# A transformer pair of blocks with expert routing: one 64-column product a token in place of two of 32, and the sum of the two halves moved off TensorE

## The reference

```
v1, i1 = top_k(s1, 16); v2, i2 = top_k(s2, 16)      # 8 heads, 128 keys each
sv, si = top_k(v1[:, None] + v2[None, :], 16)
expert = e1 * 128 + e2;  gate = softmax(sv)
a   = gelu(x . exp_u[expert])
out = sum over heads and picks of  gate * a * exp_v[expert]
```

## Time and profile before

| | |
|---|---|
| median of 3 runs | 3306.38 us (3305.8 to 3314.76) |
| profiled execution, its own time | 3306.54 us |
| its span | 3304.8 us |
| TensorE products busy | 3179.6 us, 96% |
| VectorE busy | 2340.2 us, 71% |
| ScalarE busy | 1256.1 us, 38% |
| chain that ended last | PE 67%, DVE 17%, DMA 10%, issue 4%, ACT 1% |
| read from HBM | 814.00 MB, 248 GB/s |

### The profile page before, as it was taken

The page is one execution under the profiler, slowest core; times in us unless marked ns, Lnnn a source line. Parts: engine busy times, 40 slices in busy tenths (PEclk is TensorE's granted clock), DMA queues, the critical chain, the costliest instruction groups (busy, mean ns, idle before and its releaser), DMA issues.

```text
span 3304.8 us, 71646 instructions
## 1 busy us (share of the span) xinstructions
PE 3179.6 (96%) x31390; PEld 2836.8 (86%) x31390; DVE 2340.2 (71%) x2685; ACT 1256.1 (38%) x1135; POOL 388.2 (12%) x284
## 2 busy tenths in 40 slices
PE   7999999999999989988989999999999999999998
PEld 4777768899999979988879998888888888888887
DVE  8596145799999877777779877578667766555554
ACT  2010143445444434333434444444443444443332
POOL 0276000000011222232212000200000000000000
PEclk8999999999999989999999999999999999999999
DMA  9657795546678988888788875556555566565553
GB/s 411 250 224 294 291 387 213 171 179 242 202 269 305 342 327 316 314 335 311 293 287 315 317 262 196 198 197 203 191 197 199 173 209 202 198 201 201 202 202 116
DMA packets 105301, 821.57 MB, mean 249 GB/s; under 512 B 12394, under 2 KB 14458, under 8 KB 15552
## 3 DMA queue, kind: packets, MB, share of 16 engines
q1 hardware_dynamic: 86112, 700.49, 58.4%
q0 software_dynamic: 16656, 115.53, 9.1%
q10 hardware_dynamic: 2304, 2.10, 0.2%
HBM read 814.00 MB, written 4.06 MB: 248 GB/s over the span
## 4 chain that ended last, share of the span: by engine, by line
PE 67%; DVE 17%; DMA 10%; issue 4%; ACT 1%; POOL 0%; ACTq 0%; DVEq 0%; SPq 0%; POOLq 0%
PE psW L587 17%; PE psW L588 17%; PE psW L589 17%; DVE ring L1191 7%; PE psW L585 7%; DMA ring<-wst_dram 4%; DMA arena<-urow_dram,rs 3%; DMA proj<-vrow_dram,rs 3%; DVE arena L1668 1%; PE psM L729 1%; PE psW L729 1%; PE psM L883 1%; PE psM L658 1%; ACT ring L2028 1%; DVE proj L1722 1%
## 5 line engine op out<-in xcount | busy, mean ns | idle before, releaser
L1191 DVE SCALAR_TENSOR_TENSOR ring<-ring 128x2048 f16<-128x2048 f32 x526 | 1200.3, 2294 | 522.8 <-ACT ring L2028 521.2
L2028 ACT ACTIVATE ring<-ring 128x2048 f16<-128x2048 f32 x526 | 1000.8, 1907 | 937.2 <-PE psW L589 776.5
L587 PE MATMUL psW<-h_act,ring 128*128 128x256 f16 (+1 forms) x5040 | 1339.7, 266 | 17.9 <-DVE ring L1191 13.0
L588 PE MATMUL psW<-h_act,ring 128*128 128x256 f16 (+1 forms) x5040 | 1338.8, 266 | 0.0
L589 PE MATMUL psW<-h_act,ring 128*128 128x256 f16 (+1 forms) x5040 | 1338.7, 266 | 0.0
L587 PE MATMUL psW<-arena,ring 128*128 128x208 f16 (+1 forms) x3072 | 800.0, 260 | 10.1 <-DVE ring L1191 5.6
L588 PE MATMUL psW<-arena,ring 128*128 128x208 f16 (+1 forms) x3072 | 799.6, 260 | 0.0
L589 PE MATMUL psW<-arena,ring 128*128 128x208 f16 (+1 forms) x3072 | 799.4, 260 | 0.0
L587 PEld LDWEIGHTS psW<-h_act,ring 128*128 128x128 f16 x5040 | 495.4, 98 | 81.1 <-issue 19.9
L589 PEld LDWEIGHTS psW<-h_act,ring 128*128 128x128 f16 x5040 | 495.6, 98 | 35.0
L588 PEld LDWEIGHTS psW<-h_act,ring 128*128 128x128 f16 x5040 | 495.6, 98 | 34.8
(11 more groups left out here) (405 smaller groups left out, 2584.7 us busy)
## 6 DMA issues: line engine op xcount, KB each, us to landing
ring<-wst_dram SPq DMA_DIRECT2D x522, 1024.0 KB
ring<-wst_dram SPq DMA_DIRECT2D x72, 2048.0 KB, 11.3
proj<-h_rows POOLq DMA_DIRECT2D x6, 1024.0 KB
x_res<-xT_dram POOLq DMA_DIRECT2D x2, 2048.0 KB, 17.5
out_dram<-x_res SPq DMA_DIRECT2D x4, 512.0 KB, 2.9
bias_rows<-proj POOLq DMA_DIRECT2D x1, 1536.0 KB, 21.8
x_res<-cmat_dram POOLq DMA_DIRECT2D x1, 1024.0 KB, 7.5
x_res<-bmat_dram ACTq DMA_DIRECT2D x8, 128.0 KB, 2.7
```

The lines of the kernel that those rows point to most:

```text
L587: nc.tensor.matmul(out, whi(s, col, P), xh, start=first, stop=False)
L588: nc.tensor.matmul(out, whi(s, col, P), xl, start=False, stop=False)
L1191: ins = stt(wlo(s, c, n), ring[:, s * UNIT + c:s * UNIT + c + n], WSCALE, whi(s, c, n), ALU.mult, ALU.subtract)
L2028: act(whi(s, p2 * (UNIT // 2), UNIT // 2), ring[:, c], ACT.Copy, scale=WSCALE).then_inc(hi_done, 1)
```

## The change

The two products of a token become one: its moving operand is both halves of `hot1` at once, 64 columns, and nothing is accumulated. A step then fills 1024 columns, which are both PSUM banks, so it waits until the sums of the step directly before have been taken (`sums_taken`). ScalarE first copies the sums of the low half from PSUM to `gated_w`. VectorE's `gated` waits for that copy (`low_sums`), adds the sums of the high half to it, waits for its own addition, and then multiplies as before, now with both operands in SBUF. ScalarE takes over from VectorE the waits for TensorE (`hot_used`) and for the buffer (`acts_ready`).

```diff
-        def routed(b):
-            return psM[:, b, :].rearrange("p (t e) -> p e t", t=STEP_T)
+        gate_sums = psM[:, 0:2, :].rearrange("p b (t r e) -> p (b t) r e", r=2, e=QUART_T)
+        def sums(r):
+            return gate_sums[:, :, r, :].rearrange("p t e -> p e t")
...
-                pe_.wait_ge(route_used, n + 1)
+                if n:
+                    pe_.wait_ge(sums_taken, n)
                 for t in range(STEP_T):
-                    for r in range(2):
-                        mm = nc.tensor.matmul(psM[:, b, t * QUART_T:(t + 1) * QUART_T], hot2[b][:, t, :], hot1[b][:, t, r, :],
-                                              start=(r == 0), stop=(r == 1))
+                    mm = nc.tensor.matmul(gate_sums[:, t, :, :], hot2[b][:, t, :], hot1[b][:, t, :, :], start=True, stop=True)
                 mm.then_inc(hot_used, 1)
...
             def gated(q, n):
-                v.wait_ge(hot_used, STEPS * q + n + 3)
-                if q or n >= 2:
-                    v.wait_ge(acts_ready, STEPS * q + n - 1)
-                stt(gated_w((STEPS * q + n) % 2), routed((STEPS * q + n) % 2), 1 / GSCALE, acts[:, q % 2, :, STEP_T * n:STEP_T * (n + 1)],
+                i = STEPS * q + n
+                v.wait_ge(low_sums, i + 1)
+                tt(gated_w(i % 2), sums(0), gated_w(i % 2), ALU.add).then_inc(sums_taken, 1)
+                v.wait_ge(sums_taken, i + 1)
+                stt(gated_w(i % 2), gated_w(i % 2), 1 / GSCALE, acts[:, q % 2, :, STEP_T * n:STEP_T * (n + 1)],
                     ALU.mult, ALU.mult).then_inc(route_used, 1)
...
             def route_high(q, n):
+                i = STEPS * q + n
+                a.wait_ge(hot_used, i + 3)
+                if i >= 2:
+                    a.wait_ge(acts_ready, i - 1)
+                act(gated_w(i % 2), sums(1), ACT.Copy).then_inc(low_sums, 1)
                 a.wait_ge(route_used, STEPS * q + n + 3)
                 act(routed_half(q, n, 0), gated_w((STEPS * q + n) % 2), ACT.Copy).then_inc(route_hi, 1)
```

More of the change, by code:

```diff
@@ L476, in program @@
         hot2_ready, hot1_ready, hot_used, route_used = sem("hot2_ready"), sem("hot1_ready"), sem("hot_used"), sem("route_used")
+        low_sums, sums_taken = sem("low_sums"), sem("sums_taken")
         pooled, pool_ps, pool_sb = sem("pooled"), sem("pool_ps"), sem("pool_sb")
```

## The result

The changed kernel takes 3335.21 us (median of 4 runs, 3332.43 to 3338.12), the kernel before 3306.09 beside it (4 runs). The medians lie 29 us apart. The ratio is 1.0082, 95% interval 1.0063 to 1.0101, which is 27 us more (21 to 33). The forecast was 3329, 22.7 more. The profiled execution took 3332.43 us, 25.9 more than that of before.

What follows compares the result with a forecast made beforehand. VectorE was taken to fill the routing's first quarter, neither engine the middle, both nearly the last stage. Terms of +9.4, +8.0 and +5.3 made +22.7 us on 3306.54: 3329 us, range 3309 to 3341.

Steps and rivals of the forecast that it cites:

- TensorE's step: Routing products: 16 of 64 columns at 29.2 ns, 0.47 us a step, 0.34 us saved, only where TensorE is on the chain.
- The other estimate: Routing products, from the Trainium skill: 54 ns a pair, 0.87 us a step, nothing shed, time some 3 us longer.
- VectorE's step: At `gated`: the add and its wait hold VectorE 0.72 us more a step; ends 0.60 and 0.9.
- The new wait of TensorE: Each step's products wait for the sums of the step before: a few us in the first quarter, counted at nothing.
- First quarter: Routing from 866 to 1020 us, VectorE full: 13 steps at 0.72 us, +9.4 us.
- a sign that I named: The first down-products' start, near 1018 us before, was to come 9 us later.
- The middle: Routing from 1020 to 1700 us: 13 x 0.72 less 4 x 0.34 us, +8.0 us.
- The hidden-middle rival: From 1020 to 1700 us the DMA engines hide VectorE's delay: the middle gives 0, total 3321 us; chance 0.20.
- The last routing stage: Routing from 1700 to 1860 us: 6 steps at 0.72 us, +4.3, and +1 for the rest.
- Every step pays: Rival for the whole routing: all 52 steps cost 0.72 us, +37.4 us, 3344 us; chance 0.12.
- TensorE paces the middle: Rival for 1020 to 1700 us: 26 steps save 0.34 us each, total +5.9 us, 3312 us; chance 0.13.
- TensorE everywhere: Rival for the whole routing: VectorE's add is hidden at every step, 17.7 us come off, 3289 us; chance 0.05.

Runs made afterwards that it cites:

- the run with it alone: Kernel before, but ScalarE copies the accumulated sums out of PSUM and VectorE scales them from SBUF behind that wait: 3308.79 us, ratio 1.0006.
- the run with the copy there alone: Kernel before plus a VectorE copy of the sums out of PSUM, only in the 26 steps of the middle quarters: 3314.08 us, ratio 1.0025.
- the run with VectorE's part alone: Kernel before, but VectorE first copies the sums out of PSUM, waits, then scales them from SBUF at each step: 3333.09 us, ratio 1.0080.

## Why the prediction was right

- **TensorE's step.** Forecast 29.2 ns a product and 0.47 us a step; measured 29 ns and 0.47 us. The other estimate, 54 ns and nothing shed, is out. That the saving counts only where TensorE is on the chain fits: with the buffer's wait beside it, it brought 2 us of 17.7, where the sum has 1.4 us for it in the middle.
- **VectorE's step.** Forecast 0.72 us; the timeline has 0.72. The pair of 128 elements carried over to 512. I called it a dependent pair; L1624 doesn't read what L1622 writes, but it does wait for its semaphore, and so the 0.03 us is the right row for the wait.
- **ScalarE.** Forecast 0.6 us and hidden; 0.582 us and hidden, shown by the run with it alone. The copies sum to 30.3 us, but ScalarE's busy time rose by only 24.2: the copy shown above starts at 951.40 and the `hi` half ahead of it ends at 951.50, which over 52 steps is 5 us counted once.
- **The new wait of TensorE.** Forecast a few us in the first quarter and no cost; 16.8 us over the kernel, more than I thought, 5.5 of it in the last quarter, where I expected none. Where the buffer alone was taken away the wait was 6.0 us and the cost too small to measure, 7 us at most. The other 11 us of wait come only with the rest of the change; that VectorE's lateness makes them is likely and not shown by itself.
- **First quarter.** Forecast +9.4 over 13 steps; +8.8 over the 12 intervals between its first and last add, 0.73 each. The first down-product, a sign that I named, started at 1018.38 before and 1024.58 after: 6.2 us later and not 9, because this execution was 3.3 us ahead at step 0; counted from there it is 9.5.
- **The middle.** Forecast +8.0; +8.2 in the trace, +8.3 by the run with the copy there alone, with 5.0 to 11.2 in its interval. The hidden-middle rival is out. That the three agree to 0.3 us is luck: the run with VectorE's part alone has +5.2 in its trace, and the measure moves by several us between executions. So half of the steps on the chain is a count that came out, not a rule that was shown.
- **The last routing stage: the term that was mis-sized.** Forecast 4.3 + 1; measured +10.0 in the trace and +13.2 (8.6 to 17.9) by the run. I counted 6 steps because the chain of before passed through VectorE at 6 of 13, and I gave the other steps 1 us though I had written that VectorE's 7.4 us of idle time couldn't hold 9.4 us. In fact it held next to nothing: of 7.4 us, 6.9 are still idle after. Some 4.0 us of it lie ahead of the stage's first step, and 3.2 in the last two, where VectorE waits for ScalarE's work behind `gated`; those waits move along with the delay and keep their length. Before, then after:

```profile
1837.83 0.69 DVE L1740 TENSOR_TENSOR arena<-work,arena 128x512 f16<-128x512 f32 x1 [0.70 <-ACT arena L2255]
1839.63 2.29 DVE L1191 SCALAR_TENSOR_TENSOR ring<-ring 128x2048 f16<-128x2048 f32 x1 [1.11 <-ACT ring L2028]
```

```profile
1861.55 0.69 DVE L1743 TENSOR_TENSOR arena<-work,arena 128x512 f16<-128x512 f32 x1 [0.70 <-ACT arena L2263]
1863.35 2.29 DVE L1193 SCALAR_TENSOR_TENSOR ring<-ring 128x2048 f16<-128x2048 f32 x1 [1.11 <-ACT ring L2031]
```

The chain after passes through L1735 at all 13; the first and the last are these:

```profile
1724.02 0.61 DVE work L1735
...
1875.14 0.61 DVE work L1735
```

The chain of before counts the steps at which VectorE was already last. At five of the last seven it ran through TensorE's routing products, and yet these seven too fell 0.62 to 0.75 us further behind each: VectorE had no idle time between them that could take up the delay. This term makes up 4.7 of the 6 us between the forecast and the median; the rest is within the spread of runs.

- **The other rivals.** Every step pays (+37.4 us), TensorE paces the middle (+5.9) and TensorE everywhere (a gain of 17.7) all lie outside the measured 21 to 33 us. The first was right about the last quarter and wrong about the middle.

## What to carry to other kernels

Before an addition or an evacuation is moved from TensorE to VectorE, look at which engine fills each stage, not the whole span: here TensorE was 96% busy and 17.7 us less of it were worth nothing that could be measured, while 0.72 us more of VectorE at 52 steps cost 27 us. To size such an edit, count the steps on the chain, but give a stage in which two engines are nearly full the price of all its steps, and count the delayed engine's idle time as cover only where it lies between the steps: here 4.0 us lay ahead of the first step and 3.2 us behind the delayed work itself. And when a stage belongs to VectorE, the gain lies in the shape of its operands: making f16 operands two elements contiguous in every input and output cut three instructions from 0.69 to 0.42 us and one from 2.29 to 1.22, at no cost on TensorE.

## What the runs showed of the hardware

- A two-input VectorE instruction on f16 ran at nearly twice the rate when each innermost run, in the output and both inputs, was two elements long, with the pair repeated (step zero) over the next dimension: 1219 ns against 2293 for 128x2048. With an input that repeats one element along the innermost run it went at the rate of f32: 690 ns for 128x512, against 682 for the add in f32. With runs of 16 elements it took 417, as with runs of two.
- TensorE read its moving f16 operand at full pace with a step of 4 bytes (25 ns for 32 columns) but not with 32 bytes (60 ns for 32 columns). Weights with a step of 4 bytes loaded without delaying the products of 32 columns, 25 ns apart. Between 4 and 32 bytes nothing was tried.
- An operand in PSUM made no difference to a two-input VectorE instruction of 128x512 f32: the scaling product took 693 ns with the sums in PSUM and 692 with both inputs in SBUF (the changed kernel).
- A VectorE instruction that waited for its predecessor's semaphore started 0.72 us after it at 128x512 f32, and without the wait the next one started 0.60 to 0.61 us after: the wait costs 0.11 to 0.12 us here.
